# A two-layer hybrid model on one core: the odd mixer's units in another order, and products of constants placed in TensorE's waits

## The chip, the cores and the metric

The kernel runs on one NeuronCore of a Trainium2 chip, in one launch. The metric is the device time in microseconds (us), from the program's start to its end; lower is better. The time before is the median of three runs, 2744.92 us.

TensorE (PE in the profile) multiplies matrices and writes to PSUM, an accumulator memory of eight banks. VectorE (DVE) and ScalarE (ACT) read PSUM and do element-wise work. SyncE (SP) issues the weight transfers. Each engine runs its own list of instructions strictly in the order in which the program wrote it, and waits at counters (semaphores) for the others.

## The reference

A residual stream `x` of 256 tokens by 1024 features passes through two layers of one model and two of another, all in fp32:

```python
# first block: layer 0 uses even_mixer, layer 1 uses odd_mixer; after each a mixture of experts
x = x + mix(rms_norm(x, g))
x = x + hier_moe(rms_norm(x, g), ...)      # 32 experts, hidden width 512, each token uses 2
# second block, twice
h = h + hybrid_mixer(rmsnorm(h, w), ...)
h = h + swiglu(rmsnorm(h, w), ...)
```

The change lies mostly in `odd_mixer`. Its input is projected once (`u = h @ w_in`, 2048 columns) and split into queries, keys, values and an input of a state-space part:

```python
q = apply_rope(rms_norm(q, q_norm), cos, sin)      # 4 heads x 2 halves x 64
k = apply_rope(rms_norm(k, k_norm), cos, sin)
o = softmax(q1 k1) @ v - lam * softmax(q2 k2) @ v  # causal
o_attn = rms_norm(o, subln) * (1 - lam_init)
# S5: complex diagonal recurrence over time, 2048 states, then
z = gelu(real(C @ states) + d_skip * u)
o_ssm = z * sigmoid(z @ w_glu)
return concatenate([o_attn, o_ssm]) @ w_out
```

## The kernel before

Nine stages follow each other: `even`, `moe0`, `odd`, `moe1`, `hyb0`, `ffn0`, `hyb1`, `ffn1`, `fin`. There is no planner: for every stage and every engine a function (`odd_pe`, `odd_act`, `odd_dve` and so on) writes the instructions out in order. At the end of such a function stands a list of calls to small helpers, and this list is the order of the work. A wait names an event of another engine (`K.after("odd normed0")`), or the landing of a weight chunk.

**Weights** come in chunks of 2 MB through a ring of six slots, in a fixed order on the SP queue (`sp_program`). A chunk's transfer is issued when the chunk that held its slot was used, and the chunks behind it wait as well. A mixture of experts reads all its 32 experts, 96 chunks; eight groups of four experts each have four gate chunks, four up chunks and four down chunks.

**PSUM banks** are handed out in turn by `bank`. In `odd` the banks 0 to 3 (`K.low`) and 4 to 7 (`K.high`) are two such rings; who takes a bank waits until the result that was in it four takes ago has been read.

**The mixture of experts** (`moe_pe`): the stream is transposed (L717), the router's product is taken (L785, 36 columns wide), VectorE picks the experts, and TensorE waits for that at `chosen`. Three products that count tokens follow (L789 to L791), then `gather(0)`, which collects the tokens of four experts (L804), then the weights' products: L828 for gate and up, L853 for down, L860 to spread results back over the tokens. The next stage's norm is `norm_pe` (L641): 16 transposes, eight for each half of the tokens, of which four wait for VectorE (`xv`) and four for ScalarE (`xa`). Of a transpose the trace has one record, of every fp32 product two.

**The odd mixer.** On TensorE: `inputs(j)` L1846, a quarter of the S5 input; `states(q)` L1858, a quarter of the states; `outputs(q)` L1867, a quarter of the S5 output, from what VectorE's scans gave; `query_key(i, j)` L1818, half of the queries (i = 0) or keys (i = 1); `squares(i)` L1881 and `turn(i)` L1891, their norm's sums and the rotation for the position coding; `values(t)` L1898. Then for each head h and half of the queries q, numbered n = 2h + q: `scores(n)` L1909, `transposed(n)` L1917, and per head `weighted(h)` L1925 and L1926. `head_squares` L1933 sums for the heads' norm, `gate()` is the product of the S5 gate (again L1818), and `out(n, first)` L1956 the output projection: for each of four blocks of the result four products over the S5 half (`first`), then four over the heads' half.

On VectorE: `turned_in(q)`, six operations over 128x1024; `scanned(q)`, eight scans over time (L2182) and four such operations; `outputs(q)` L2192; `normed(i)` L2200; `roped(i)` from L2207 on; `largest(n)` and `weighed(n)`, the row maxima and the softmax weights; two operations of the GELU (L2268 and L2273, called cubic and gelu); L2282, called mixed, which applies the gate; `heads(j)` L2244. On ScalarE: the readings of PSUM, `rstd(i)`, `exp(n)`, the GELU's square and tanh (L2098, L2102), the gate's tanh (L2115) and `head_rstd(j)` (L2077, L2080).

The waits that matter below: `turn(i)` waits for `normed(i)`; `turned_in(q)` waits for `states(q)` and, before its second half, for `outputs(q-1)` of TensorE; `scores(0)` waits for `roped(1)`; `gate` for gelu; `mixed` for both halves of the gate; `out(n, True)` for mixed; `heads(j)` for `head_rstd(j)`.

## Time and profile before

| | us |
|---|---|
| runs before | 2742.62, 2744.92, 2747.47 (median 2744.92) |
| the profiled execution, its own time | 2738.76 |
| its span, first to last instruction | 2737.0 |
| `even` | 0 to 271.9 |
| `moe0` | 271.9 to 737 |
| `odd` | 737 to 910 |
| `moe1` | 910 to 1375 |
| both hybrid layers, their feed-forwards, the last norm | 1375 to 2737 |
| busy over the span | TensorE 84%, VectorE 46%, ScalarE 34% |
| mean granted TensorE clock | 0.936 |

A clock of 1.00 is 2.4 GHz and 0.50 is 1.2 GHz; the trace shows only these two levels, and a mean between them is a stretch in which it changed. The profile's lines on the granted clock and on the transfers, 40 slices of 68.4 us each, show the stages: in the two mixtures of experts the 16 DMA engines are busy all the time (428 GB/s), in `odd` they are nearly idle for one slice (17 GB/s), and in the second block they run at a third to a half of that rate while TensorE is busy.

The times in the stretches below are us from the span's start. In a timeline a row merges neighbouring instructions of one line: start, length, engine, line, operation, then how many records (x16), and in brackets how long the engine stood idle before it and who released it.

### The profile page before, as it was taken

The page shows a single profiled execution, that of the slowest core. Times are in us where ns is not written, and L with a number is a line of the kernel's source. Part 1 is how long each engine was busy: PE and PEld are TensorE (multiplying, and loading weights), DVE is VectorE, ACT ScalarE, POOL GpSimd, SP SyncE. Part 2 cuts the span into 40 slices and gives each one's busy share as a digit, 9 for nine tenths or more (in the row PEclk, how much of TensorE's full clock was granted, in tenths as well). Part 3 has the DMA queues.
Part 4 walks back from the last instruction along what each step waited for, and adds up shares of the span by engine and source line. Part 5 has one row for each costly group of instructions (what it writes and reads, how often), then busy time and mean ns, then how long its engine had stood idle before and what let it go on. Part 6 is the DMA issues. An engine that isn't in the chain of part 4 may idle for free.

```text
span 2737.0 us, 37411 instructions
## 1 busy us (share of the span) xinstructions
PE 2300.2 (84%) x16364; PEld 1749.6 (64%) x16364; DVE 1263.6 (46%) x1914; ACT 941.2 (34%) x1382; POOL 2.4 (0%) x8
## 2 busy tenths in 40 slices
PE   7877766666696866666599999999999999999999
PEld 6666322211274421122189998999979999989997
DVE  2575321222294211111066568765545656866554
ACT  3133100000113200000055557745444555764543
POOL 0000000000000000000000000000000000000000
PEclk9998888988897988878899999999999999999999
DMA  6101999999905599999954443445544434334452
GB/s 274 62 1 74 400 428 428 428 427 428 416 17 248 244 428 427 427 428 428 427 198 170 149 178 141 154 154 199 182 172 154 167 146 185 130 148 160 180 185 100
DMA packets 47818, 663.18 MB, mean 242 GB/s; under 512 B 5280, under 2 KB 5536, under 8 KB 7584
## 3 DMA queue, kind: packets, MB, share of 16 engines
q1 hardware_dynamic: 47072, 657.39, 59.7%
q8 instruction: 132, 2.16, 0.3%
q0 software_dynamic: 576, 3.32, 0.3%
q14 instruction: 38, 0.31, 0.0%
HBM read 659.64 MB, written 1.05 MB: 241 GB/s over the span
## 4 chain that ended last, share of the span: by engine, by line
PE 54%; DMA 29%; DVE 9%; ACT 7%; issue 2%; SPq 0%; DVEq 0%; ACTq 0%
DMA ring<-w_dram 28%; PE ps L2346 7%; PE ps L2348 7%; PE ps L2347 7%; PE ps L1818 3%; PE ps L1231 2%; PE ps L828 2%; PE ps L2599 2%; PE ps L2600 2%; PE ps L2601 2%; PE ps L853 2%; ACT r L2323 2%; PE ps L3201 1%; PE ps L3199 1%; PE ps L3200 1%
## 5 line engine op out<-in xcount | busy, mean ns | idle before, releaser
L2334 DVE TENSOR_TENSOR r<-ring,r 128x1024 fp32r<-128x1024 f32 (+1 forms) x392 | 505.1, 1301 | 345.9 <-ACT r L2323 345.3
L2346 PE MATMUL ps<-r 128*128 128x256 f32 x2112 | 608.0, 288 | 15.1 <-DVE arena L2933 5.7
L2347 PE MATMUL ps<-r 128*128 128x256 f32 x2112 | 598.2, 283 | 0.0
L2348 PE MATMUL ps<-r 128*128 128x256 f32 x2112 | 598.0, 283 | 0.0
L2323 ACT ACTIVATE r<-ring 128x1024 fp32r<-128x1024 f32 (+1 forms) x392 | 429.5, 1116 | 269.1 <-PE ps L2348 131.8
L828 PE MATMUL ps<-ring,arena 128*32 128x512 f32 x1984 | 297.4, 731 | 207.0 <-DMA ring<-w_dram 206.9
L2346 PEld LDWEIGHTS ps<-r 128*128 128x128 f32 x2112 | 405.5, 192 | 22.8 <-issue 6.7
L2347 PEld LDWEIGHTS ps<-r 128*128 128x128 f32 x2112 | 405.7, 192 | 0.2
L2348 PEld LDWEIGHTS ps<-r 128*128 128x128 f32 x2112 | 405.5, 192 | 0.0
L828 PEld LDWEIGHTS ps<-ring,arena 128*32 128x32 f32 x1984 | 62.1, 121 | 433.0 <-DMA ring<-w_dram 221.2
L1030 DVE TENSOR_TENSOR arena<-ps,arena 128x512 f32<-128x512 f32 x16 | 11.1, 692 | 472.7 <-PE ps L828 472.7
L853 PE MATMUL ps<-ring,arena 128*32 128x512 f32 x1024 | 145.4, 702 | 81.1 <-DMA ring<-w_dram 80.1
L2599 PE MATMUL ps<-arena,r 128*128 128x256 f32 x512 | 145.4, 284 | 0.0
L2600 PE MATMUL ps<-arena,r 128*128 128x256 f32 x512 | 143.9, 281 | 0.0
L853 PEld LDWEIGHTS ps<-ring,arena 128*32 128x32 f32 x1024 | 30.5, 119 | 177.2 <-DMA ring<-w_dram 121.8
L2601 PE MATMUL ps<-arena,r 128*128 128x256 f32 x512 | 143.8, 281 | 0.0
L878 ACT ACTIVATE arena<-ps 128x512 f32<-128x512 f32 x16 | 9.6, 597 | 292.9 <-PE ps L828 292.9
L880 ACT ACTIVATE arena<-ps 128x256 f32<-128x256 f32 x16 | 6.1, 383 | 285.4 <-PE ps L834 285.4
L885 ACT ACTIVATE arena<-ps 128x512 f32<-128x512 f32 x16 | 9.6, 597 | 262.7 <-PE ps L853 262.7
L1038 DVE COPY arena<-ps 128x512 f32<-128x512 f32 x16 | 11.1, 692 | 192.4 <-PE ps L853 192.4
L2599 PEld LDWEIGHTS ps<-arena,r 128*128 128x128 f32 x512 | 96.5, 188 | 1.2 <-issue 0.7
L2600 PEld LDWEIGHTS ps<-arena,r 128*128 128x128 f32 x512 | 96.5, 188 | 0.1
(433 smaller groups left out, 3416.6 us busy)
## 6 DMA issues: line engine op xcount, KB each, us to landing
ring<-w_dram SPq DMA_DIRECT2D x305, 2048.0 KB, 23.7
arena<-w_dram SPq DMA_DIRECT2D x4, 2048.0 KB, 21.9
ring<-w_dram SPq DMA_DIRECT2D x4, 1024.0 KB, 4.9
cst<-w_dram POOLq DMA_DIRECT2D x2, 973.0 KB, 8.2
x<-x_dram SPq DMA_DIRECT2D x1, 1024.0 KB, 7.9
ring<-w_dram SPq DMA_DIRECT2D x2, 512.0 KB, 13.5
out_dram<-x SPq DMA_DIRECT2D x4, 256.0 KB, 2.0
ring<-w_dram SPq DMA_DIRECT2D x1, 768.0 KB, 15.8
```

The costliest lines, as they stand in the source:

```text
L828: r = pe.matmul(p[32 * j:32 * j + 32, :], xg[:, k, j * CAP:(j + 1) * CAP], w[:, kk * 4 + j, :], start=k == 0, stop=k == 7)
L853: r = pe.matmul(ys[n][32 * j:32 * j + 32, :], b.HTr[u][:, k, j * CAP:(j + 1) * CAP], w[:, j, n * 512:(n + 1) * 512], start=k == 0, stop=k ...
L1231: x = pe.matmul(o(c), l[:, c, :], r(c), start=True, stop=True)
L1818: r = pe.matmul(p[:, n * 256:(n + 1) * 256], w[:, k, c0 + n * 128:c0 + n * 128 + 128], rhs[:, k, :], start=k == 0, stop=k == n_k - 1)
L2323: a.activation(hi, w, ACT.Copy).then_inc(*S.up(f"hi {s}"))
L2334: v.tensor_tensor(lo, w, hi.bitcast(F32), SUB).then_inc(*S.up(f"lo {s}", *(["free " + name] if last else [])))
L2346: pe.matmul(out, hi[:, k, :], K.HH[:, k, :], start=k == 0, stop=False)
L2347: pe.matmul(out, hi[:, k, :], K.HL[:, k, :], start=False, stop=False)
L2348: r = pe.matmul(out, lo[:, k, :], K.HH[:, k, :], start=False, stop=k == 7)
L2599: pe.matmul(o, hi[:, k, :], b.YH[:, kk, :], start=kk == 0 and n == 0, stop=False)
L2600: pe.matmul(o, hi[:, k, :], b.YL[:, kk, :], start=False, stop=False)
L2601: r = pe.matmul(o, lo[:, k, :], b.YH[:, kk, :], start=False, stop=kk == 15 and n == 1)
```

## The change

It has two parts. The first writes the odd mixer's list of calls in another order on three engines, cuts the gate's product into its two halves (`gate(0)`, `gate(2)`), cuts the heads' half of the output projection into pairs of products (`out_heads(n, j)`, which needs only `heads(j)`), and puts `normed(i)` between the two rows of scans of `scanned(2)` and `scanned(3)`. The work itself stays the same.

The second adds `warm`, a product of two constants (the identity by a part of a table that begins with it) into a PSUM bank whose contents are overwritten later. It stands ahead of waits: in `norm_pe` (stages `odd`, `hyb0`, `ffn0`, `hyb1`, `ffn1`) once before the wait for `xv0`, 512 or 256 columns wide, and twice, 128 wide, before the wait for `xv1`; three times, 512 wide, before `chosen` in both mixtures of experts; and six times, 512 wide, between the four down chunks of the last group of experts.

```diff
+def warm(K, pe, out):
+
+    n = out.shape[1]
+    pe.matmul(out, K.par("ident", 0, 128), K.par("ident", 0, n), start=True, stop=True)
...
 def norm_pe(K, pe, st):
...
                 p[k] = bank(K, pe, name, of)
             if k == 0:
+                if t == 0 and K.stage_before(st):
+                    warm(K, pe, p[0][:, 0:512 if after_moe(K, st) else 256])
+                elif t and K.stage_before(st):
+                    warm(K, pe, p[6][:, 128:256])
+                    warm(K, pe, p[6][:, 384:512])
                 pe.wait_ge(*K.after(f"{st} xv{t}"))
...
     p = bank(K, pe, st + " pos")
+    for _ in range(3):
+        warm(K, pe, p)
     pe.wait_ge(*K.after(st + " chosen"))
...
         ys = [bank(K, pe, f"{st} y{q}{n}") for n in range(2)]
+        if q == NE // 4 - 1:
+            spare = bank(K, pe, f"{st} o{q}00")
...
             r.then_inc(*S.up("free " + name, f"{st} y{q}"))
+            if q == NE // 4 - 1 and k < 3:
+                warm(K, pe, spare)
+                warm(K, pe, spare)
         for t in range(2):
             for n in range(2):
                 pe.wait_ge(*K.after(f"{st} y{q}{n} read"))
-                p = bank(K, pe, f"{st} o{q}{n}{t}")
+                p = spare if q == NE // 4 - 1 and t == n == 0 else bank(K, pe, f"{st} o{q}{n}{t}")
...
-    def gate():
+    def gate(j):
         pe.wait_ge(*K.landed("glu"))
         pe.wait_ge(*K.after("odd gelu"))
-        for j in (0, 2):
-            for _ in proj_T_pe(K, pe, S, "glu", j * 128, b.Y5, 4, f"odd glu{j}", j == 2, K.high):
-                pass
+        for _ in proj_T_pe(K, pe, S, "glu", j * 128, b.Y5, 4, f"odd glu{j}", j == 2, K.high):
+            pass
...
-    def out(n, first):
+    def out(n, ready, ks):
 
         i, t = divmod(n, 2)
         w = K.chunk(f"odd_out{i}")
-        if first:
+        if ks[0] == 4:
             pe.wait_ge(*K.landed(f"odd_out{i}"))
             acc[n] = bank(K, pe, f"odd out{i}{t}", K.low)
-            pe.wait_ge(*K.after("odd mixed"))
-        else:
-            pe.wait_ge(*K.after("odd heads2"))
-        for k in range(4, 8) if first else range(4):
+        pe.wait_ge(*K.after(ready))
+        for k in ks:
             r = pe.matmul(acc[n], b.OT[:, k, t * 128:(t + 1) * 128], w[:, k, :], start=k == 4, stop=k == 3)
-        if not first:
+        if ks[-1] == 3:
             r.then_inc(*S.up(f"odd out{i}{t}", f"free odd_out{i}"))
+
+    def out_states(n):
+        out(n, "odd mixed", range(4, 8))
+
+    def out_heads(n, j):
+        out(n, f"odd heads{j}", range(j, j + 2))
 
     inputs(0)
     states(0)
@@ -1966,48 +1987,54 @@
     outputs(0)
     query_key(0, 2)
     inputs(3)
+    states(2)
     squares(0)
-    states(2)
+    outputs(1)
     turn(0)
-    outputs(1)
     query_key(1, 0)
     states(3)
     query_key(1, 2)
     outputs(2)
+    squares(1)
     values(0)
-    squares(1)
+    turn(1)
     values(1)
-    turn(1)
     outputs(3)
     scores(0)
     scores(1)
     scores(2)
+    scores(3)
     transposed(0)
-    scores(3)
+    scores(4)
+    gate(0)
     transposed(1)
     weighted(0)
-    scores(4)
+    scores(5)
+    gate(2)
     transposed(2)
-    scores(5)
+    scores(6)
     transposed(3)
     weighted(1)
-    scores(6)
+    scores(7)
+    transposed(4)
     head_squares(0)
-    gate()
-    transposed(4)
-    scores(7)
     transposed(5)
     weighted(2)
-    out(0, True)
+    out_states(0)
     transposed(6)
-    out(1, True)
+    out_states(1)
     transposed(7)
     weighted(3)
-    out(2, True)
+    out_states(2)
     head_squares(2)
-    out(3, True)
-    for n in (0, 2, 1, 3):
-        out(n, False)
+    out_states(3)
+    out_heads(0, 0)
+    out_heads(2, 0)
+    out_heads(0, 2)
+    out_heads(2, 2)
+    for n in (1, 3):
+        out_heads(n, 0)
+        out_heads(n, 2)
 
...
 def odd_act(K, a, st):
...
+    def gate(j):
+        a.wait_ge(*K.after(f"odd glu{j}"))
+        a.activation(b.U5[:, j:j + 2, :], half2(K.high[f"odd glu{j}"]), ACT.Tanh).then_inc(*S.up(f"odd glu{j} read"))
...
     rstd(0)
     query_key(1, 0)
     query_key(1, 2)
+    rstd(1)
     values(0)
-    rstd(1)
     values(1)
-    exp(0)
-    exp(1)
     a.wait_ge(*K.after("odd y3"))
     a.wait_ge(*K.after("odd normed1"))
     a.activation(b.RS, b.Y5, ACT.Square).then_inc(*S.up("odd y squares"))
-    exp(2)
-    transposed(0)
+    exp(0)
+    exp(1)
     a.wait_ge(*K.after("odd cubic"))
     a.activation(b.RS, b.RS, ACT.Tanh, scale=4 * GELU * 16 * 0.044715).then_inc(*S.up("odd tanh"))
+    transposed(0)
+    exp(2)
+    gate(0)
+    transposed(1)
     exp(3)
-    transposed(1)
     weighted(0)
     exp(4)
+    gate(2)
     transposed(2)
+    transposed(3)
     exp(5)
-    transposed(3)
     weighted(1)
     exp(6)
-    head_rstd(0)
-    for j in (0, 2):
-        a.wait_ge(*K.after(f"odd glu{j}"))
-        a.activation(b.U5[:, j:j + 2, :], half2(K.high[f"odd glu{j}"]), ACT.Tanh).then_inc(*S.up(f"odd glu{j} read"))
     transposed(4)
-    exp(7)
     transposed(5)
     weighted(2)
+    exp(7)
+    head_rstd(0)
     transposed(6)
     transposed(7)
     weighted(3)
...
 def odd_dve(K, v, st):
...
         tt(b.TB, b.TB, b.TA, SUB)
         own()
 
-    def scanned(q):
+    def scanned(q, which=None):
 
         Y, Z = b.Y[q % 2], b.Z[q % 2]
         for x in (Y, b.TB):
             for i in range(4):
                 r = bc(s.rho[:, q * 4 + i:q * 4 + i + 1], [128, 256])
                 v.tensor_tensor_scan(x[:, i, :], r, x[:, i, :], 0.0, MUL, ADD).then_inc(*S.up())
+            if x is Y and which is not None:
+                normed(which)
         own()
         tt(b.TA, Y, s.CS[q], MUL)
         v.scalar_tensor_tensor(out=Z, in0=b.TB, scalar=-1.0, in1=s.SN[q], op0=MUL, op1=MUL).then_inc(*S.up())
@@ -2249,28 +2281,26 @@
     turned_in(1)
     scanned(1)
     outputs(0)
-    normed(0)
     turned_in(2)
+    outputs(1)
+    scanned(2, 0)
     roped(0)
-    scanned(2)
-    outputs(1)
     turned_in(3)
-    scanned(3)
     outputs(2)
-    normed(1)
+    scanned(3, 1)
     roped(1)
     outputs(3)
     largest(0)
     largest(1)
-    weighed(0)
-    largest(2)
     v.wait_ge(*K.after("odd y squares"))
     v.scalar_tensor_tensor(out=b.RS, in0=b.RS, scalar=1.0 / (16 * 0.044715), in1=b.Y5, op0=ADD, op1=MUL).then_inc(
         *S.up("odd cubic"))
+    weighed(0)
+    largest(2)
+    v.wait_ge(*K.after("odd tanh"))
+    v.scalar_tensor_tensor(out=b.Y5, in0=b.RS, scalar=1.0, in1=b.Y5, op0=ADD, op1=MUL).then_inc(*S.up("odd gelu"))
     weighed(1)
     largest(3)
-    v.wait_ge(*K.after("odd tanh"))
-    v.scalar_tensor_tensor(out=b.Y5, in0=b.RS, scalar=1.0, in1=b.Y5, op0=ADD, op1=MUL).then_inc(*S.up("odd gelu"))
     weighed(2)
     largest(4)
     weighed(3)
```

What the lists make of it, at three places. The rows are the programs' instructions in order, without times: line, operation, what it writes and reads, the shape of the output, and how many alike follow. Lines of the changed file are its own.

TensorE, the projections of the odd mixer, from `inputs(3)` (L1846) on, before: `squares(0)` L1881, `states(2)` L1858, `turn(0)` L1891, `outputs(1)` L1867, then `query_key`, `states(3)`, `query_key`, `outputs(2)`, `values(0)` L1898, `squares(1)`, `values(1)`:

```order
L1846 MATMUL ps<-ring 128x256 x8
L1881 MATMUL ps<-arena,pp 128x256 x4
L1858 MATMUL ps<-arena,ring 128x256 x8
L1891 MATMUL ps<-arena,cst 128x256 x4
L1867 MATMUL ps<-arena,ring 32x256 x16
L1818 MATMUL ps<-ring 128x256 x16
L1858 MATMUL ps<-arena,ring 128x256 x8
L1818 MATMUL ps<-ring 128x256 x16
L1867 MATMUL ps<-arena,ring 32x256 x16
L1898 MATMUL ps<-ring 128x512 x8
L1881 MATMUL ps<-arena,pp 128x256 x4
L1898 MATMUL ps<-ring 128x512 x8
```

and now, the same helpers at L1864, L1899, L1876, L1909, L1885, L1836 and L1916:

```order
L1864 MATMUL ps<-ring 128x256 x8
L1876 MATMUL ps<-arena,ring 128x256 x8
L1899 MATMUL ps<-arena,pp 128x256 x4
L1885 MATMUL ps<-arena,ring 32x256 x16
L1909 MATMUL ps<-arena,cst 128x256 x4
L1836 MATMUL ps<-ring 128x256 x16
L1876 MATMUL ps<-arena,ring 128x256 x8
L1836 MATMUL ps<-ring 128x256 x16
L1885 MATMUL ps<-arena,ring 32x256 x16
L1899 MATMUL ps<-arena,pp 128x256 x4
L1916 MATMUL ps<-ring 128x512 x8
L1909 MATMUL ps<-arena,cst 128x256 x4
```

`states(2)` (L1876) stands ahead of `squares(0)` (L1899), `outputs(1)` (L1885) ahead of `turn(0)` (L1909), and the second `turn` ahead of the second `values`.

VectorE, from the end of `outputs(0)` (L2192) to the scans of the third quarter (L2182), before; L2200 is `normed(0)`, L2207 the start of `roped(0)`:

```order
L2192 SCALAR_TENSOR_TENSOR arena<-arena,cst,ps 128x256
L2200 SCALAR_TENSOR_TENSOR arena<-arena,pp 128x1024
L2134 TENSOR_TENSOR arena<-ps,arena 128x1024 x2
L2134 TENSOR_TENSOR arena<-arena 128x1024
L2134 TENSOR_TENSOR arena<-ps,arena 128x1024 x2
L2134 TENSOR_TENSOR arena<-arena 128x1024
L2207 TENSOR_TENSOR arena<-ps,cst 128x512 x2
L2134 TENSOR_TENSOR arena<-arena,cst 128x1024
L2134 TENSOR_TENSOR arena<-arena 128x1024
L2182 SCALAR_TENSOR_TENSOR arena<-cst,arena 128x256 x8
```

and now, with `outputs` at L2224, scans at L2212 and `normed(0)` at L2232; `roped(0)` is at L2239:

```order
L2224 SCALAR_TENSOR_TENSOR arena<-arena,cst,ps 128x256
L2164 TENSOR_TENSOR arena<-ps,arena 128x1024 x2
L2164 TENSOR_TENSOR arena<-arena 128x1024
L2164 TENSOR_TENSOR arena<-ps,arena 128x1024 x2
L2164 TENSOR_TENSOR arena<-arena 128x1024
L2224 SCALAR_TENSOR_TENSOR arena<-arena,cst,ps 128x256
L2212 SCALAR_TENSOR_TENSOR arena<-cst,arena 128x256 x4
L2232 SCALAR_TENSOR_TENSOR arena<-arena,pp 128x1024
L2212 SCALAR_TENSOR_TENSOR arena<-cst,arena 128x256 x4
L2164 TENSOR_TENSOR arena<-arena 128x1024
L2217 SCALAR_TENSOR_TENSOR arena<-arena 128x1024
L2218 SCALAR_TENSOR_TENSOR arena<-arena 128x1024
```

`normed(0)` was the first thing after `outputs(0)`; it now stands seven operations and four scans later, and `roped(0)` behind all eight scans and their four products.

TensorE, attention, from `scores(6)` on, before: `head_squares(0)` L1933, the whole gate L1818, transposes L1917, `weighted(2)` L1925 and L1926, `out(0, True)` L1956:

```order
L1909 MATMUL ps<-arena 128x128 x2
L1933 MATMUL ps<-arena,pp 128x256 x2
L1818 MATMUL ps<-arena,ring 128x256 x16
L1917 MATMUL ps<-pp,arena 128x128
L1909 MATMUL ps<-arena 128x256 x2
L1917 MATMUL ps<-pp,arena 128x128 x2
L1925 MATMUL ps<-arena 128x256
L1926 MATMUL ps<-arena 128x128
L1956 MATMUL ps<-ring,arena 128x512 x4
```

and now, from `scores(3)` on, with `scores` at L1927, transposes L1935, the gate's halves L1836, `weighted(0)` at L1943 and L1944:

```order
L1927 MATMUL ps<-arena 128x256 x2
L1935 MATMUL ps<-pp,arena 128x128
L1927 MATMUL ps<-arena 128x128 x2
L1836 MATMUL ps<-arena,ring 128x256 x8
L1935 MATMUL ps<-pp,arena 128x128 x2
L1943 MATMUL ps<-arena 128x256
L1944 MATMUL ps<-arena 128x128
L1927 MATMUL ps<-arena 128x256 x2
L1836 MATMUL ps<-arena,ring 128x256 x8
L1935 MATMUL ps<-pp,arena 128x128
L1927 MATMUL ps<-arena 128x128 x2
```

The gate's first half stands between the transposes of the first head, the second half ahead of those of the second head; before, both stood behind the second head.

## Rows read from the trace of the kernel before

**Rows 1.** The page, chain that ended last, by engine.
```profile
PE 54%; DMA 29%; DVE 9%; ACT 7%; issue 2%; SPq 0%; DVEq 0%; ACTq 0%
```

**Rows 2.** Stretches: length, busy and instructions by engine, PE clock, DMA share, GB/s.
```profile
841.00:910.00 69.00, 54.58 (x166) 30.32 (x163) 24.79 (x67) 28.47 (x72) 0.00 (x0) 0.80 0.61 252
880.00:905.00 25.00, 24.29 (x61) 11.11 (x61) 2.13 (x3) 8.73 (x16) 0.00 (x0) 0.97 0.02 9
921.00:930.00 9.00, 9.00 (x64) 7.16 (x68) 4.12 (x17) 0.00 (x0) 0.00 (x0) 0.73 0.01 4
```

**Rows 3.** Timeline of PE, projections of the odd mixer (start, length, ..., idle before).
```profile
782.36 1.92 PE L1881 MATMUL ps<-arena,pp 128*128 128x256 f32 x4 [3.06 <-DVE arena L2192]
...
792.64 7.17 PE L1818 MATMUL ps<-ring 128*128 128x256 f32 x32
...
818.94 1.89 PE L1881 MATMUL ps<-arena,pp 128*128 128x256 f32 x8
826.80 8.88 PE L1898 MATMUL ps<-ring 128*128 128x512 f32 x16 [5.98 <-DVE arena L2192]
...
840.67 0.93 PE L1909 MATMUL ps<-arena 64*128 64x128 f32 x8 [1.40 <-DVE arena L2134]
```

**Rows 4.** Timeline of DVE, the same stretch.
```profile
772.49 4.77 DVE L2182 TENSOR_TENSOR_SCAN arena<-cst,arena 128x256 f32<-128x256 f32 x8
...
781.83 0.48 DVE L2192 SCALAR_TENSOR_TENSOR arena<-arena,cst,ps 128x256 f32<-128x256 f32 x1
787.49 1.28 DVE L2200 SCALAR_TENSOR_TENSOR arena<-arena,pp 128x1024 f32<-128x1024 f32 x1 [5.18 <-ACT arena L2046]
788.69 2.35 DVE L2134 TENSOR_TENSOR arena<-ps,arena 128x1024 f32<-128x1024 f32 x2
...
836.58 0.69 DVE L2207 TENSOR_TENSOR arena<-ps,cst 128x512 f32<-128x512 f32 x1 [8.64 <-PE ps L1891]
```

**Rows 5.** Timeline of PE, attention, gate and output projection.
```profile
862.94 7.84 PE L1818 MATMUL ps<-arena,ring 128*128 128x256 f32 x32
...
875.73 1.19 PE L1925 MATMUL ps<-arena 128*128 128x256 f32 x2 [3.84 <-ACT arena L2065]
...
892.29 17.74 PE L1956 MATMUL ps<-ring,arena 128*128 128x512 f32 x40
```

**Rows 6.** Timeline of DVE, the wait for the gate.
```profile
871.44 1.23 DVE L2282 SCALAR_TENSOR_TENSOR arena<-arena 128x1024 f32<-128x1024 f32 x1 [8.13 <-ACT arena L2115]
```

**Rows 7.** Stretch of DVE: largest(4), weighed(3), largest(5), weighed(4).
```profile
853.60:858.10 4.50, 4.21 (x14) 0.50 1.01 433
```

**Rows 8.** Stretch of ACT: head_rstd(0), four instructions.
```profile
863.20:867.20 4.00, 3.88 (x4) 0.84 1.01 426
```

**Rows 9.** Timeline of ACT, the first of them.
```profile
863.20 1.28 ACT L2077 ACT_TABLE_LOAD   x1
```

**Rows 10.** Stretches of PE: length, busy, granted clock, DMA share, GB/s.
```profile
277.50:287.50 10.00, 6.27 (x28) 0.50 1.00 425
728.00:731.40 3.40, 3.34 (x16) 0.51 0.97 408
844.00:864.50 20.50, 12.53 (x38) 0.50 1.01 429
```

**Rows 11.** Timeline of PE, first mixture of experts: after the router, gather(0), gather(1).
```profile
280.41 0.60 PE L789 MATMUL ps<-arena,pp 128*128 128x32 f32 x2 [3.29 <-DVE arena L970]
...
282.69 6.16 PE L804 MATMUL ps<-arena 128*128 128x128 f32 x32 [0.82 <-issue]
...
304.46 3.74 PE L804 MATMUL ps<-arena 128*128 128x128 f32 x32
```

**Rows 12.** Timeline of PE, its last group: two down chunks, the next norm.
```profile
723.17 1.92 PE L853 MATMUL ps<-ring,arena 128*32 128x512 f32 x16 [1.59 <-DMA ring<-w_dram]
728.06 3.53 PE L853 MATMUL ps<-ring,arena 128*32 128x512 f32 x16 [2.97 <-DMA ring<-w_dram]
...
738.84 1.50 PE L641 MATMUL ps<-pp,arena 128*128 128x128 f32 x12 [0.70 <-ACT arena L576]
```

## The prediction

> **What bounds the kernel now.** I read the chain of waits first: TensorE holds 54% of it, transfers 29% [rows 1]. The transfers' share lies in the two mixtures of experts, whose weights run at full rate. So I asked what lies between them, the odd mixer, and whether time saved there survives. Stretches of the page answer the second question: between 880 and 905 us the DMA engines are idle (share 0.02), and again between 921 and 930 (0.01) [rows 2]. The next weights wait there for a slot, which TensorE frees when it reaches the experts. What the odd mixer ends earlier, `moe1` starts and ends earlier, as long as it is less than these 34 us.
>
> Then the timelines, engine against engine. In the projections both engines wait in turn. TensorE waits 3.06 us at 782.36 inside `squares(0)`, whose second bank is free only after VectorE's `outputs(0)`, with `states(2)` queued behind it; and 5.98 us at 826.80, `values(1)`, for the bank that VectorE's `outputs(2)` reads [rows 3]. VectorE waits 5.18 us for the norm's factors before `normed(0)` and 8.64 us before `roped(1)`, for `turn(1)`, which stands behind `values(1)` [rows 4]. In attention TensorE does the whole gate in one piece, 7.84 us, and meanwhile VectorE waits 8.13 us for it at `mixed` [rows 5, 6]; after that TensorE waits 3.84 us for the third head [rows 5]. Only then does the output projection begin. From 841 to 910 TensorE is busy 54.6 us at a mean clock of 0.80 [rows 2]; between 844 and 864.5 it is at 0.50 throughout [rows 10].
>
> **The projections.** All before `squares(0)` is as it was. I follow the new lists with the old durations: 3.5 us for `inputs` or `states` (half of the 7.17 us of a `query_key`), 1.9 us for `outputs`, 1.75 for `squares` or `turn`, 7.0 for `values` at full clock [rows 3]; on VectorE 1.15 to 1.18 us for an operation over 128x1024, so 7.1 for `turned_in`, 4.8 for eight scans, 9.4 for `scanned` [rows 4].
>
> `states(2)` now ends at 781.8, before VectorE is through with `outputs(0)` at 782.3. VectorE therefore goes straight into `turned_in(2)`: the 5.18 us go. It ends at 789.5, `outputs(1)` at 789.9, four scans at 792.3, and `normed(0)` at 793.4. This is 5 us later than before, and it is the new wait: TensorE is through with `outputs(1)` at 785.5, and `turn(0)` blocks it for 8 us. Everything behind it is queued: `query_key(1, 0)`, `states(3)`, `query_key(1, 2)`, `outputs(2)`. The clock will have fallen; I add 1.4 us. From there TensorE alone sets the pace: turn 1.75, query_key 7, states 3.5, query_key 7, outputs 1.9, squares 1.75, values 7, turn 1.75, values 7, outputs 1.9, in all 40.5, plus 1.4: it ends at 835.4. VectorE fits beside it: `scanned(2)` ends at 800.5, `roped(0)` at 804.2, then it waits for `states(3)` to 807.1 and in the middle of `turned_in(3)` for `outputs(2)` to 816.0, so `normed(1)` is done at 823.6, `scanned(3)` at 830.6, `roped(1)` at 834.3. `scores(0)` starts at 835.4 instead of 840.67 [rows 3]: 5.3 us gained. The margins are 1.2 us (`turn(1)` wants `normed(1)` at 824.8) and 1.1 us (`roped(1)`). Ends: 1.4 us less if the clock stays up; 3.5 more if it is low until the first `query_key` is done.
>
> **Attention.** VectorE's work up to `mixed` is `largest` and `weighed` for n = 0 to 5, one more `largest`, and three GELU and gate products. Two pairs of the former take 4.5 us [rows 7], so 13.5, plus 1.1, plus three of 1.2 [rows 6] make 18.2 us. It is ready at 835.9, and would end at 854.1 without a wait. I find 5 us of waits. Half of the gate, 3.5 us at full clock and 7 at the low one, starts at 843.0 when gelu is there; TensorE has been nearly idle by then, and I take 5.7 us, to 848.7. `transposed(1)` stands behind it, and behind that on ScalarE `exp(3)`, so VectorE waits some 3 us before `weighed(3)`. The second half of the gate ends at 854.5, and `scores(6)`, behind it, costs 0.7 more, `exp(5)` behind the gate's tanh another 0.7. `mixed` is done at 859.4, and the output projection begins at 860.0, with `weighted(2)` just ahead. Before, it began at 877.3.
>
> From there: four `out_states` and four times `out_heads`, 3.44 us for four products (17.74 us for five times as many at full clock [rows 5]), 27.5 us; the transposes, `weighted(3)` and `head_squares(2)` 1.8; and about 1.6 of waiting for `weighed(7)`. For ScalarE does `head_rstd(0)` after `exp(7)`, 3.9 us [rows 8], `heads(0)` waits for that, and `weighed(7)` stands behind `heads(0)`. That gives 890.9, plus 1.2 for low clock at the start of `out_states(0)`: 892.1. `head_rstd(2)` lies beside `out_states(3)` as before. Against the old 910.0 this is 17.9 us less for the whole stage, of which 12.6 in attention. Ends: 1.2 less with the clock up; 8 more if both halves of the gate (another 1.3 and 3.5) and more of the output projection run low.
>
> Here a page speaks against the new order. Rows first: ScalarE's load of tables takes 1.28 us [rows 9], and the two loads and two operations of `head_rstd` 3.9 in all [rows 8]. The Trainium skill, "ScalarE: Activation LUTs", section "What ACT_TABLE_LOAD costs", adds about 1.4 us of draining to each switch, 2.66 in all. By that rule `head_rstd(0)` would hold `weighed(7)` 2.8 us longer, and the stage would end 2.8 us later. The trace has no such gap.
>
> **The products of constants.** A 512-column fp32 product takes 0.86 us at 1.00 (a fourth of 3.44) and twice that at 0.50.
> - Ahead of `chosen`, three: 2.6 us warm, 5.2 cold, in a wait of 3.29 us [rows 11]. The clock was at 0.50 from 277.5 to 287.5 [rows 10]; `gather(0)` took 6.16 us, `gather(1)` at full clock 3.74 [rows 11]. Best case: hidden, gather 2.4 us shorter, the small products 0.4. Worst: all at the low level, 1.9 us late, and gather no faster. I take 1.0 us gained, nearer the best, because three dense products in a row are what preceded each rise of the clock here. Two stages: 2.0.
> - In the last group of experts, two after each of three down chunks, 1.72 us in a gap of 3 [rows 12]. The last chunk ran at 0.50 [rows 10] and took 3.53 us instead of 1.92 [rows 12]; `moe1` shows the same. Gain 1.6 and 1.4 in this execution. If the first chunk starts cold, 3.5 + 3.5 us exceed the 4.9 between chunks, which is caught up by the fourth. Ends: nothing, and these 3.0.
> - In the norms, one in a wait of over a microsecond: free. Two of 128 columns, 0.43 us together, stand ahead of `xv1`, which in `odd` is long there: the eight transposes behind them move 0.43 us [rows 12], and the chain with them. In `hyb0` 0 to 0.9, I take 0.4, since the cutting of weights lies beside. In `ffn0`, `hyb1`, `ffn1` `xv1` comes last: nothing.
>
> **Sum.** Against the profiled execution's 2738.76: -17.9 (odd) -2.0 -3.0 +0.4 +0.4 = -22.1. The median of the runs lies 6.2 us above the profiled one, and whether a last chunk meets the low clock will vary from run to run, so I count half of the 3.0: 2744.92 - 20.6 = 2724.
>
> **Rivals.**
> A. The constants run cold and late. For: the clock was low just there. Against: it rises after dense work [rows 10, 11]. Both `chosen` 1.9 late instead of 1.0 early, and no gain at the last chunks: 2724 + 5.8 + 1.5 + 1 for the norms = 2732.
> B. Attention keeps most of its length, because the gate's half ahead of `transposed(1)` holds back every later softmax at low clock, and only the projections gain: of the 12.6 us 3 remain. For: the cold stretch [rows 10]. 2724 + 9.6 = 2734.
> C. The stream of weights takes the gain: `moe1` ends when it did. Against: 34 us of idle DMA [rows 2]. Only the first mixture's gain would stay: 2742.
> D. Slower. From 842 to the end of the stage the clock stays at 0.50, because the work is chopped into pieces between waits. TensorE has 40 us of work there, which then costs 40 more, less the 3.4 already counted: 2724 + 36.6 = 2761. It decides from 21 us of the work at the low level beyond those counted. For: in this stretch it was low for 20.5 us [rows 10]. Against: the gate and the output projection are long dense pieces, and each ran at full clock after its beginning. The Trainium skill, "TensorE: Matmul & The Clock Gate", section "A second HAM failure mode: psum-queue depth-cycling", tells of a kernel that idled briefly between groups and swung between the levels; by that rule this rival would be likelier than I make it.
>
> **How the numbers follow.** Forecast 0.70, A 0.12, B 0.09, C 0.05, D 0.04. The forecast's own ends are 2717 (everything at full clock) and 2736 (the projections' 3.5 and the attention's 8 us); A and B lie inside. I give 2716 to 2737. A measurement of this kernel can tell about 0.2%, 5.5 us. Forecast, A and B are faster by more, and a few of their tails are not: faster 0.91, within 0.2% 0.05 (C), slower 0.04 (D).
>
> **What would show it.** In the profile after: VectorE without a wait before `turned_in(2)`; TensorE idle for 8 us before `turn(0)`; `scores(0)` 5 us sooner after the norm than before; the gate in two pieces with VectorE's wait at `mixed` gone and one of about 3 us before `weighed(3)`; the output projection starting 17 us earlier; gather(0) near 3.7 us; the last down chunk at 1.9 us. It is wrong if `mixed` comes later than 25 us after `scores(0)`, or if `moe1` is longer than before.

## The result and the profile after

| | before | after |
|---|---|---|
| median of the runs timed together, us | 2743.77 (4 runs, 2742.60 to 2747.47) | 2716.53 (4 runs, 2712.74 to 2718.73) |
| the profiled execution, its own time | 2738.76 | 2717.73 |
| its span | 2737.0 | 2715.9 |
| mean granted TensorE clock | 0.936 | 0.943 |

The ratio after to before is 0.9897, with a 95% interval of 0.988 to 0.9914, so the change takes 24 to 33 us off. The medians differ by 27.2 us, the two profiled executions by 21.0. Forecast were 20.6 and 22.1. The direction came as forecast, and so did the odd mixer; the products of constants gave more than was counted. The gain against the median is a third larger than forecast, and 2716.53 lies half a microsecond above the lower end of the range.

The timeline of TensorE in the kernel after, from the odd mixer's projections to the output projection:

```profile
780.73 1.89 PE L1899 MATMUL ps<-arena,pp 128*128 128x256 f32 x8
782.55 1.93 PE L1885 MATMUL ps<-arena,ring 128*32 128x256 f32 x32
792.49 3.75 PE L1909 MATMUL ps<-arena,cst 128*128 128x256 f32 x8 [8.01 <-issue]
796.03 7.21 PE L1836 MATMUL ps<-ring 128*128 128x256 f32 x32
...
834.64 0.93 PE L1927 MATMUL ps<-arena 64*128 64x128 f32 x8
...
841.97 6.42 PE L1836 MATMUL ps<-arena,ring 128*128 128x256 f32 x16 [1.25 <-issue]
...
850.85 3.72 PE L1836 MATMUL ps<-arena,ring 128*128 128x256 f32 x16
...
860.20 3.60 PE L1971 MATMUL ps<-ring,arena 128*128 128x512 f32 x8
...
868.03 0.41 PE L1935 MATMUL ps<-pp,arena 128*128 128x128 f32 x2 [0.69 <-DVE arena L2270]
...
891.20 1.92 PE L728 MATMUL ps<-pp,x 128*128 128x128 f32 x16
```

The new wait is there: 8.01 us before `turn(0)` (L1909). The profile names no releaser for it ("issue"), but by the list `turn(0)` waits for `normed(0)`, and VectorE ends that at 792.38, 0.11 us before `turn(0)` starts. The gate (L1836) stands in two pieces of 6.42 and 3.72 us where it was one of 7.84 [rows 5]. The output projection (L1971) begins at 860.20; it began at 877.14.

VectorE's timeline after, at `outputs(0)` and `turned_in(2)`, then its longer waits further on:

```profile
780.82 0.47 DVE L2224 SCALAR_TENSOR_TENSOR arena<-arena,cst,ps 128x256 f32<-128x256 f32 x1
781.22 2.34 DVE L2164 TENSOR_TENSOR arena<-ps,arena 128x1024 f32<-128x1024 f32 x2
...
791.12 1.26 DVE L2232 SCALAR_TENSOR_TENSOR arena<-arena,pp 128x1024 f32<-128x1024 f32 x1
...
806.73 2.35 DVE L2164 TENSOR_TENSOR arena<-ps,arena 128x1024 f32<-128x1024 f32 x2 [3.74 <-PE ps L1876]
815.53 2.36 DVE L2164 TENSOR_TENSOR arena<-ps,arena 128x1024 f32<-128x1024 f32 x2 [5.19 <-PE ps L1885]
...
850.30 0.17 DVE L2265 RECIPROCAL cst<-cst 128x2 f32<-128x2 f32 x1 [4.02 <-ACT arena L2085]
...
866.08 0.75 DVE L2276 SCALAR_TENSOR_TENSOR arena<-arena,cst 128x512 f32<-128x512 f32 x1 [4.53 <-ACT arena L2107]
```

The wait of 5.18 us behind `outputs(0)` [rows 4] is gone, and so are the one of 8.64 before `roped(1)` [rows 4] and the one of 8.13 at `mixed` [rows 6]. What has come instead in attention is 4.02 us before `weighed(3)` and 4.53 us before `heads(0)` (L2276), which waits for `head_rstd(0)`. The waits of 3.74 and 5.19 cost nothing, since TensorE works without a pause from 792.49 to the end of `outputs(3)`.

ScalarE's timeline after, `head_rstd(0)` (L2104 and L2107):

```profile
862.04 1.28 ACT L2104 ACT_TABLE_LOAD   x1
863.34 0.69 ACT L2104 ACTIVATE arena<-ps,pp 128x512 f32<-128x512 f32 x1
864.04 1.28 ACT L2107 ACT_TABLE_LOAD   x1
865.34 0.63 ACT L2107 ACTIVATE arena<-arena 128x512 f32<-128x512 f32 x1
```

Stretches of TensorE after: length, busy and records, granted clock, share of the DMA engines, GB/s:

```profile
279.80:289.00 9.20, 7.85 (x54) 1.00 1.02 432
785.00:797.00 12.00, 4.51 (x12) 0.72 0.00 0
...
840.00:848.00 8.00, 6.72 (x20) 0.57 1.01 426
848.00:890.00 42.00, 38.83 (x127) 1.00 0.70 293
...
902.00:905.50 3.50, 3.50 (x19) 0.52 0.02 9
```

In the first mixture of experts nothing is at the low level from 279.8 on, where it was from 277.5 to 287.5 [rows 10]. In attention the low level lasts some 7 us in 840 to 848; before, it lasted 20.5 [rows 10] and another 6.8 us from 874.7 to 881.5. Over the whole stage, from `inputs(0)` to `moe1`, the mean granted clock is 0.95 instead of 0.89, and TensorE is busy 135.2 us instead of 143.4 with the same instructions. So about 8 of the 17.7 us between these two profiles are the same work at a higher clock, and the rest is less waiting. The kernel with the new order alone (below) has the same two numbers, 0.95 and 134.8 us.

TensorE's timeline after, first mixture: the three products of constants (L630, two records each) and `gather(0)` (L817); the same in the second mixture; then the last group's down chunks (L868):

```profile
279.81 2.82 PE L630 MATMUL ps<-pp 128*128 128x512 f32 x6
...
284.84 3.81 PE L817 MATMUL ps<-arena 128*128 128x128 f32 x32 [0.82 <-issue]
...
896.45 2.82 PE L630 MATMUL ps<-pp 128*128 128x512 f32 x6
...
901.48 5.44 PE L817 MATMUL ps<-arena 128*128 128x128 f32 x32 [0.82 <-issue]
```

```profile
713.63 2.96 PE L868 MATMUL ps<-ring,arena 128*32 128x512 f32 x16 [1.52 <-DMA ring<-w_dram]
716.52 2.60 PE L630 MATMUL ps<-pp 128*128 128x512 f32 x4
...
728.22 1.92 PE L868 MATMUL ps<-ring,arena 128*32 128x512 f32 x16 [1.05 <-DMA ring<-w_dram]
```

`gather(0)` went from 6.16 to 3.81 us [rows 11], in the second mixture only to 5.44. The last down chunk went from 3.53 to 1.92 [rows 12].

Before and after by stage, in us, from the starts of the same instructions in the traces. Two more executions of the kernel before were profiled later, and the column of before has all three:

| stretch | before, three executions | after |
|---|---|---|
| `even`, up to the first mixture | 271.7, 275.6, 272.5 | 274.6 |
| first mixture to its first weights' product | 17.44, 17.72, 17.34 | 14.39 |
| from there to `inputs(0)` of `odd` | 451.60, 452.51, 451.04 | 450.79 |
| `odd`, from `inputs(0)` to the transposes of `moe1` | 169.11, 169.07, 169.62 | 151.46 |
| second mixture to its first weights' product | 17.51, 17.25, 17.48 | 16.01 |
| from there to the first product of `hyb0` | 452.63, 452.92, 452.92 | 451.32 |
| the second block to the end | 1357.00, 1359.28, 1359.41 | 1357.37 |

`even` differs by up to 4 us between executions of one kernel, and the change touches nothing in it.

### The profile page after: what moved, and what is told of

It reads as the page before. It is cut to its first block, busy times and chain, and to the rows that moved or that the text cites. A ratio compares the mean times of both kernels' runs of the same rounds, so it can differ in the third digit from the quotient of the medians.

```text
span 2715.9 us, 37536 instructions
## 1 busy us (share of the span) xinstructions
PE 2311.1 (85%) x16430; PEld 1755.8 (65%) x16430; DVE 1263.2 (47%) x1914; ACT 941.1 (35%) x1382; POOL 2.4 (0%) x8
## 3 DMA queue, kind: packets, MB, share of 16 engines
q0 software_dynamic: 576, 3.32, 0.3%
## 4 chain that ended last, share of the span: by engine, by line
PE 56%; DMA 29%; ACT 7%; DVE 6%; issue 2%; SPq 0%; DVEq 0%; ACTq 0%
DMA ring<-w_dram 29%; PE ps L2376 7%; PE ps L2377 7%; PE ps L2378 7%; PE ps L1836 4%; PE ps L1249 2%; PE ps L841 2%; PE ps L2629 2%; PE ps L2630 2%; PE ps L2631 2%; ACT r L2353 2%; PE ps L868 2%; PE ps L3229 1%; PE ps L3231 1%; PE ps L3230 1%
## 5 line engine op out<-in xcount | busy, mean ns | idle before, releaser
L868 PE MATMUL ps<-ring,arena 128*32 128x512 f32 x1024 | 141.1, 684 | 67.6 <-DMA ring<-w_dram 66.6
L868 PEld LDWEIGHTS ps<-ring,arena 128*32 128x32 f32 x1024 | 30.2, 117 | 158.9 <-DMA ring<-w_dram 102.7
```

Of the source, the lines that this page charges most:

```text
L868: r = pe.matmul(ys[n][32 * j:32 * j + 32, :], b.HTr[u][:, k, j * CAP:(j + 1) * CAP], w[:, j, n * 512:(n + 1) * 512], start=k == 0, stop=k ...
```

## The experiments

The order of the lists and the products of constants are taken apart first, then the constants by place; then come the waits that the new order left.

**The new order alone.** The changed kernel with every call of `warm` out, and with the first spreading product's bank taken where it was before.

```diff
-                    warm(K, pe, p[0][:, 0:512 if after_moe(K, st) else 256])
...
-                    warm(K, pe, p[6][:, 128:256])
-                    warm(K, pe, p[6][:, 384:512])
...
-    for _ in range(3):
-        warm(K, pe, p)
...
-                warm(K, pe, spare)
-                warm(K, pe, spare)
```

> The changed kernel without any product of constants. Measured for the whole change: 27.2 us less by the medians (0.9897), where 20.6 were forecast. Theory A (the constants are worth more than the 3 us I gave them): the order alone gives the 17.5 us that the timelines show for the odd stage, ratio 0.9936, some 2726 us. Theory B (the constants are sized right, the order gives more than its stage shows): 24 us, ratio 0.9912, some 2720 us.

Measured: 2724.25 (2722.67 to 2727.09) against 2741.48 for before on the same chip, ratio 0.9933 [0.992, 0.9946], which is 18.4 us less (14.8 to 21.9). From `inputs(0)` to `moe1` it is 150.74 us, against 151.46 with the constants. So the order is worth what was forecast for it, 17.9 us, and no more. It also shortens the stretch from `moe1`'s transposes to its first weights' product without any constants, to 16.55 us from some 17.4.

One thing was not expected. The timeline of TensorE in this kernel, last down chunk of the second mixture and the four products that spread it (L866), and the stretch around them:

```profile
1349.02 3.64 PE L859 MATMUL ps<-ring,arena 128*32 128x512 f32 x16 [1.74 <-DMA ring<-w_dram]
1353.38 6.17 PE L866 MATMUL ps<-arena 128*128 128x512 f32 x8 [0.72 <-ACT arena L891]
```

```profile
1342.00:1363.00 21.00, 14.36 (x51) 0.67 0.90 383
```

The clock is low at the end of `moe1`, and its last four products take 6.17 us instead of 3.70. From the first weights' product to `hyb0` it is 455.49 us, 2.7 more than in the three executions of before. The new order is not shown to be the cause. The kernel without the six products (below) has the new order and nothing in these waits either, and there the four products take 3.70 us. And one of the later executions of the kernel before has the same in its first mixture:

```profile
735.70 5.44 PE L860 MATMUL ps<-arena 128*128 128x512 f32 x8 [0.70 <-ACT arena L885]
```

Without the six products the four ran partly at the low level in two of ten places (two mixtures in each of five profiles); with them, in none of eighteen.

**The products of constants alone.** The kernel before with all of `warm`, its lists in the old order.

```diff
+def warm(K, pe, out):
+    n = out.shape[1]
+    pe.matmul(out, K.par("ident", 0, 128), K.par("ident", 0, n), start=True, stop=True)
...
+    for _ in range(3):
+        warm(K, pe, p)
...
+            if q == NE // 4 - 1 and k < 3:
+                warm(K, pe, spare)
+                warm(K, pe, spare)
```

> The kernel before with all products of constants, and its old order. Theory A: 9 to 10 us less, ratio 0.9965. Theory B: 3 us less, ratio 0.999. If both parts act independently, this ratio and that of the order alone multiply to 0.9897.

Measured: 2734.72 (2729.51 to 2736.99), ratio 0.9967 [0.9955, 0.9979]: 9.1 us less (5.8 to 12.3). The prediction counted 2.0 + 1.5 - 0.8 = 2.7. The two ratios multiply to 0.9900, the whole change gave 0.9897: the parts add up within the intervals, and this one was mis-sized. By stages, against the mean of the three executions of before, it has 3.1 and 1.4 us in the two stretches to the first weights' product, 1.3 and 1.5 in the rest of the two mixtures, and 0.7 in the odd mixer.

**Without the six in the last group.**

```diff
-            if q == NE // 4 - 1 and k < 3:
-                warm(K, pe, spare)
-                warm(K, pe, spare)
```

> The changed kernel without the six products in the last group of experts. I sized them at 3.0 us in the profiled execution and half of it in the median. Theory A, if they are the underrated part: 4 us or more slower than the changed kernel (ratio to before 0.9912 or more), and last down chunks at 3.4 us. Theory B: 1.5 us slower, ratio 0.9902.

Measured: 2721.61 (2718.63 to 2721.93), ratio 0.992 [0.9907, 0.9933], 5.1 us above the whole change by medians, 6.3 by the ratios to before. The two intervals overlap at the edge, so the runs alone do not prove this size; the stages show the place. The last down chunk of the second mixture takes again over 3 us:

```profile
1346.38 3.38 PE L866 MATMUL ps<-ring,arena 128*32 128x512 f32 x16 [2.97 <-DMA ring<-w_dram]
```

From the first weights' product to this row's start it is 438.82 us; in all fourteen profiled executions of this case that distance lies between 438.49 and 438.85, with the six products and without. The transfers set it. What the six products give is only what comes behind the last transfer: the last chunk's own time, the spreading products, the norm. To `hyb0` it is 454.06 us here, 451.3 to 451.6 in the nine executions with the six. Of these 2.7 us the last chunk has 1.5 and its later start 0.3. The rest, 1.0, is a pause of 2.83 us of TensorE ahead of the norm, in this kernel's profile only, for which the profile names no cause; it is not shown to belong to the six products. What is regular is the chunk: 3.15 to 3.64 us in all ten places without the six, 1.92 in all eighteen with them, so 1.2 to 1.7 us in each mixture.

**Without the three ahead of `chosen`.**

```diff
     p = bank(K, pe, st + " pos")
-    for _ in range(3):
-        warm(K, pe, p)
     pe.wait_ge(*K.after(st + " chosen"))
```

> The changed kernel without the three products ahead of chosen, in both mixtures. Sized at 1.0 us each. Theory A, if these are the underrated part: 2.5 to 3 us each, so 5 to 6 slower than the changed kernel, ratio to before about 0.9917, and gather(0) at 6.2 us again. Theory B: 2 us slower, ratio 0.9904.

Measured: 2719.67 (2716.68 to 2724.58), ratio 0.9921 [0.9908, 0.9933], 3.1 us above the whole change by medians, 6.6 by the ratios to before. By stages: 17.41 us to the first weights' product instead of 14.39 in the first mixture, 16.70 instead of 16.01 in the second. The size is inconclusive by the runs alone, since the intervals overlap. The profiles of all kernels show the place, and that the gain is not the same each time. The first mixture's stretch is 17.3 to 17.7 us in the five without these products; in the eight with three of them it is 14.4 in six and 15.3 in two. The second's is 16.55 and 16.70 in the two with the new order and no product there; with three it is 16.0 in three, 15.3 in two and 14.4 in two.

**One product instead of three there.**

```diff
-    for _ in range(3):
+    for _ in range(1):
         warm(K, pe, p)
```

> The changed kernel with one product ahead of chosen instead of three. If the clock holds because TensorE has any dense work between the router and gather: gather(0) stays near 3.8 us in the first mixture, time as the changed kernel, ratio 0.9897. If it needs them all: gather(0) at 5.4 to 6.2 us in both and 3 to 4.5 us slower than the changed kernel, ratio 0.991.

Measured: 2716.64 (2713.89 to 2719.01), ratio 0.9903 [0.9886, 0.9919]: the same time as with three. TensorE's timeline, first mixture:

```profile
280.68 1.10 PE L630 MATMUL ps<-pp 128*128 128x512 f32 x2
...
285.71 5.15 PE L817 MATMUL ps<-arena 128*128 128x128 f32 x32 [0.82 <-issue]
```

The stage has 15.72 us to its first weights' product, between 14.39 with three and 17.41 with none, and `gather(0)` 5.15 between 3.81 and some 6.2. In the first mixture one product gives about half of the gain; in the second the stretch is 16.54 us, as without any. The runs cannot tell 1.3 us.

**Without those in the norms.**

```diff
-                if t == 0 and K.stage_before(st):
-                    warm(K, pe, p[0][:, 0:512 if after_moe(K, st) else 256])
-                elif t and K.stage_before(st):
-                    warm(K, pe, p[6][:, 128:256])
-                    warm(K, pe, p[6][:, 384:512])
```

> The changed kernel without the products in the five norms. So far: the order alone gives 0.9933, all products alone 0.9967; removing those before chosen costs 4.5 us, those of the last group 5. Theory A1 (the two groups are all of it, the norms' cost a little, as I priced them at 0.8 us): 0.5 to 1 us faster than the changed kernel, ratio to before 0.9895. Rival A2 (the norms' products also help, because in some executions the clock falls in a norm and the work behind it starts at 0.50): 1 to 3 us slower, ratio 0.9905.

Measured: 2716.44 (2714.14 to 2719.12), ratio 0.9904 [0.9887, 0.992]: no difference from the whole change. The norm ahead of `odd`, first in this kernel (transposes L647, then `inputs(0)`), then in the kernel after (L652):

```profile
738.04 0.63 PE L647 MATMUL ps<-pp,arena 128*128 128x128 f32 x4 [1.48 <-DVE arena L609]
739.37 2.79 PE L647 MATMUL ps<-pp,arena 128*128 128x128 f32 x12 [0.70 <-ACT arena L576]
741.96 4.05 PE L1859 MATMUL ps<-ring 128*128 128x256 f32 x16
```

```profile
735.95 0.66 PE L652 MATMUL ps<-pp,arena 128*128 128x128 f32 x4 [0.53 <-DVE arena L609]
737.38 0.63 PE L652 MATMUL ps<-pp,arena 128*128 128x128 f32 x4 [0.77 <-ACT arena L576]
737.85 0.61 PE L630 MATMUL ps<-pp 128*128 128x128 f32 x4
738.30 1.04 PE L652 MATMUL ps<-pp,arena 128*128 128x128 f32 x8
739.74 3.69 PE L1864 MATMUL ps<-ring 128*128 128x256 f32 x16 [0.41 <-DVE ring L664]
```

Without them twelve transposes run partly at the low level here, 2.79 us; with them four and eight take 1.67 and the two small products lie between. But the clock does not fall in every norm without them. The same twelve transposes in the kernel with the new order alone, which has no products in the norms either:

```profile
741.13 1.51 PE L647 MATMUL ps<-pp,arena 128*128 128x128 f32 x12 [0.72 <-ACT arena L576]
```

From the last spreading product to `inputs(0)` it is 4.6 to 4.7 us in three of the five profiles without these products, 5.2 and 5.4 in the two where the clock fell, and 5.2 in all nine with them. So in `odd` they cost the 0.4 to 0.5 us that were forecast, except where they keep the clock up. Ahead of `hyb0` it is 6.4 us with them, and 6.3 to 6.4 without.

This kernel also shows the other end of the products ahead of `chosen`. They stand directly behind the router, which ran at full clock, and still the clock fell while they ran; so it did in the first mixture of the next kernel, with `query_key(1, 0)` ahead of `turn(0)`, of which this is the timeline of TensorE:

```profile
277.94 4.52 PE L630 MATMUL ps<-pp 128*128 128x512 f32 x6
...
283.87 3.81 PE L817 MATMUL ps<-arena 128*128 128x128 f32 x32 [0.82 <-issue]
```

The three take 4.52 us instead of 2.82 and end after VectorE's choice is there, and the counting products start 1.0 us later than in the kernel after (9.6 instead of 8.6 us behind the first transpose of the mixture). `gather(0)` is at full clock all the same. These are the places where the stretch is 15.3 us.

**`query_key(1, 0)` ahead of `turn(0)`.** The half of the keys needs nothing that `turn(0)` waits for, and it takes 7.2 us, about the length of the new wait.

```diff
     outputs(1)
-    turn(0)
     query_key(1, 0)
+    turn(0)
     states(3)
```

> The changed kernel with query_key(1, 0) ahead of turn(0) on TensorE: the 8 us that TensorE waits for normed(0) are filled with 7 us of work. If TensorE alone sets the pace behind that wait, as I predicted from the lists: the stage 6 to 8 us shorter, ratio to before 0.987. Rival: ScalarE may read the keys only after roped(0), so their bank stays held and outputs(2) and squares(1) wait for it, VectorE becomes the bound, and 3 us or less are gained, ratio 0.989.

Measured: 2704.56 (2703.30 to 2708.74), ratio 0.9865 [0.9848, 0.9883]: 37 us less than before, and 12.0 less than the changed kernel by medians, 8.8 by the ratios to before (11.9 and 10.5 less than the kernel without the norms' products and the one with the late gate, which ran beside it on the same chip). TensorE's timeline in this kernel, and below it two stretches with their clocks:

```profile
782.51 7.17 PE L1836 MATMUL ps<-ring 128*128 128x256 f32 x32
790.60 1.97 PE L1909 MATMUL ps<-arena,cst 128*128 128x256 f32 x8 [0.91 <-issue]
...
823.97 0.93 PE L1927 MATMUL ps<-arena 64*128 64x128 f32 x8
...
831.31 5.40 PE L1836 MATMUL ps<-arena,ring 128*128 128x256 f32 x16 [0.90 <-issue]
```

```profile
782.50:800.00 17.50, 16.59 (x80) 1.00 0.00 0
829.00:837.00 8.00, 6.79 (x23) 0.64 1.02 430
```

The wait is 0.91 us instead of 8.01, and `turn(0)` takes 1.97 instead of 3.75, for the clock stays up. From `inputs(0)` to `scores(0)` it is 86.13 us against 94.90 (7.1 of the wait, 1.8 of `turn(0)`), and from `inputs(0)` to `moe1` 141.68 against 151.46, 9.8 us less. So the forecast wait was real, it was on the path, and nothing behind it hid it. Of VectorE's waits of 3.74 and 5.19 us the first went with it and 0.23 are left of the second: they were an echo of TensorE's. The rival, by which the bank of the keys would have held TensorE up and 3 us or less were gained, did not come.

**The first half of the gate behind `transposed(1)`.**

```diff
     scores(4)
-    gate(0)
     transposed(1)
+    gate(0)
     weighted(0)
     scores(5)
```

(the same on ScalarE's list, behind `exp(3)`.)

> The changed kernel with the gate's first half behind transposed(1) instead of ahead of it, on TensorE and ScalarE. The wait of 4.0 us before weighed(3) should go. If that wait is on the path to mixed: out_states(0) 2 to 3 us earlier, ratio to before 0.989. Rival: the gate then ends later by the same amount and mixed waits for it, no change against the changed kernel, 0.99.

Measured: 2715.08 (2713.22 to 2715.94), ratio 0.9901 [0.9884, 0.9918]: no difference from the whole change. VectorE's timeline in this kernel:

```profile
846.44 0.69 DVE L2252 SCALAR_TENSOR_TENSOR arena<-ps,cst 128x512 f32<-128x512 f32 x1 [3.21 <-PE ps L1927]
850.62 0.42 DVE L2252 SCALAR_TENSOR_TENSOR arena<-ps,cst 128x256 f32<-128x256 f32 x1 [1.72 <-PE ps L1927]
```

The wait of 4.02 us before `weighed(3)` is gone, and one of 3.21 stands before `largest(5)`: now `scores(5)` is queued behind the half of the gate. From `scores(0)` to the output projection it is 25.13 us, against 25.56; the kernels with the gate in its first place have 24.3 to 25.6, so this is no gain. In both places tried, something that VectorE needs is behind the half of the gate.

**All three rearrangements.** The two above, and `weighed(7)` ahead of `heads(0)`, which no longer waits then for `head_rstd(0)`.

```diff
     weighed(6)
-    heads(0)
     weighed(7)
+    heads(0)
     heads(2)
```

> Both of these, and weighed(7) ahead of heads(0) on VectorE, so that the last transposes no longer wait for ScalarE's head_rstd(0). If the three waits are independent: 7 + 2.5 + 1 us less than the changed kernel, some 2705 us, ratio 0.986. If they overlap: 0.988.

Measured: 2705.40 (2703.61 to 2705.73), ratio 0.9865 [0.9848, 0.9881]: what the first of them gives alone. The third shortens the output projection by 0.9 us (30.12 against 31.00), less than the runs can tell.

**`query_key(1, 0)` first and `weighed(7)` first,** without the move of the gate.

```diff
-    turn(0)
     query_key(1, 0)
+    turn(0)
...
-    heads(0)
     weighed(7)
+    heads(0)
```

> The changed kernel with query_key(1, 0) ahead of turn(0), and weighed(7) ahead of heads(0). The first alone gave 2704.6 us, ratio 0.9865. If weighed(7) is worth what the trace of all three together shows, 0.9 us from the start of the output projection to the next stage: 2703.5 us, ratio 0.9861. Rival: the order of weighed(7) is hidden behind out_states(1), no difference.

Measured: 2707.12 (2701.38 to 2710.05), ratio 0.9875 [0.9859, 0.9892]. No gain over 2704.56. The 0.9 us of the output projection are there again (30.13).

**The kernel before, profiled twice more.** No edit.

> The kernel before, unchanged, one more profiled execution, to see where its profiled execution of 2738.8 us was shorter than the median of 2743.8. Theory C (the forecast's own basis was a lucky execution): this one takes 2741 us or more, with the even stage 2 to 4 us longer than 271.7 and, in the second mixture, the last group's end later, 449 to 451 us from its first expert product to the next norm instead of 447.7. Rival D: the stages repeat to half a microsecond, and the 5 us lie outside the span or spread over the second block.

> The same once more. Theory C: again 2741 us or more, by the even stage and the last groups. Rival D: as the first.

Measured: 2746.14 and 2742.12, one execution each. They are 7.4 and 3.4 us longer than the profiled execution on which the sum was made. Of the 7.4, `even` has 3.9 and the second block 2.3; of the 3.4, 0.8 and 2.4. Each of the stretches that the change touches differs by at most 0.9 us from the first profile. So the profiled execution was short mostly where the change does nothing. The expected later end of the last group did not come: from the first weights' product of `moe1` to the next norm it is 448.0 us in both, against 447.7.

The version to keep is the one with `query_key(1, 0)` ahead of `turn(0)`: 2704.56 us, faster than both kernels. The two that add more moves to it cannot be told from it.

## Why the prediction was right, and where it was not

**Projections: right.** Forecast was VectorE straight into `turned_in(2)`, 8 us of waiting before `turn(0)`, 1.4 us for the clock, and `scores(0)` 5.3 us sooner after the norm. The trace has no wait, 8.01 us, 1.8 us (3.75 against 1.97 at full clock), and 94.90 us from `inputs(0)` to `scores(0)` against 99.92, 5.0 sooner.

**Attention: right.** Forecast were `out_states(0)` 24.6 us behind `scores(0)`, a first half of the gate of 5.7 us and a wait of about 3 before `weighed(3)`. Measured were 25.56, 6.42 and 4.02. The loss of 1.0 us was made up behind it: from `out_states(0)` to `moe1` forecast were 32.1 us, measured 31.00, since the 1.2 us for a low clock did not come and the 1.6 us of waiting for `weighed(7)` came to 0.69. From `inputs(0)` on the stage shrank by 17.8 us against the mean of the three executions of before; forecast were 17.9, and the kernel with the new order alone took off 18.4 (14.8 to 21.9).

By an estimate from the Trainium skill, "ScalarE: Activation LUTs", section "What ACT_TABLE_LOAD costs", two drains of about 1.4 us would have made this 2.8 us longer. The trace does not agree: `head_rstd(0)` takes 3.9 us from 862.04 to 865.97 with its loads of 1.28 us back to back with the work, as before [rows 8].

**The stream of weights: right.** The second mixture begins earlier and ends earlier, and the distance from its first weights' product to its last down chunk is the same in every kernel (438.5 to 438.9 us).

**The clock in attention: right.** Rival D wanted 0.50 up to the end of the stage; it is 1.00 from 848 to 890. Some 7 us in 840 to 848 remain.

**The step that failed: the sum for the products of constants.** It counted 2.7 us, and the runs of the constants alone gave 9.1 (5.8 to 12.3). What they do was seen rightly; the sizes of two terms were too small. In the table, less is a gain:

| term | counted | measured, by stages |
|---|---|---|
| ahead of `chosen`, first mixture | -1.0 | -3.1 in six of eight profiles (17.5 to 14.4), -2.2 in two (15.3) |
| the same, second mixture | -1.0 | -1.4 with the old order (17.4 to 16.0); with the new one -0.6 in this execution (16.6 to 16.0), -0.6 to -2.2 in all |
| last group, both mixtures | -1.5, half of 3.0 | -3.0, from the last chunks alone (some 3.4 to 1.92 each) |
| norms | +0.8 | +0.5 in `odd` where the clock stays up without them (three of five profiles), none in `hyb0` |
| together | -2.7 | -7.0 with the old order |

- For `chosen` the sum took 1.0 us out of a span from 1.9 lost to 2.8 gained. In the kernel after, and in most of the others, the first mixture got the best end and a little more: the three products follow the router at full clock, and the stretch from 279.8 to 289 is at 1.00 throughout. The worst end came nowhere, but a part of it did: in four of sixteen places the clock fell inside the three products, which then ended 1.0 us late, and the gather was fast even so. The two effects stand in one place together, where the sum had them as one or the other. The reason given for the choice, three dense products ahead of each rise of the clock, is not what the trace shows either: at 830.3 us the clock rose two products into `values(1)`.
- In the second mixture the kernel after is 1.4 us shorter, but some 0.8 of this comes from the new order: 16.55 us without any constants. The sum had no term for it.
- Halving the last group's 3.0 us was the wrong correction. All three executions of before have a cold last chunk in both mixtures (3.53, 3.15, 3.24 and 3.32, 3.60, 3.47 us), every kernel with the six products has 1.92. The gain was regular; it needed no discount. What may be saved at times behind that chunk, up to 2.5 us in the four spreading products, was not counted; two places of ten do not show that it is due to the six.
- The norms' +0.4 in `odd` was right where the clock stays up without them; the +0.4 in `hyb0` did not come.

Of the 9.1 us the stages place 7.0 in these four terms. The profile of the constants alone has another 0.7 in the odd mixer, where none of them stands. The remainder lies within the interval and has no place.

**The basis.** The sum was made on a profiled execution 6.2 us below the median and carried over to the median unchanged. That was right: `even`, which the change does not touch, and the second block, where its products in the norms show nothing, made it short. It also explains why the difference of the two profiled executions (21.0) looks like a hit on the forecast 22.1: `even` was 2.9 us longer in the one after, and that hides the larger gain of the constants. By the stages that the change touches, against the mean of the three executions of before, it is 17.8 + 3.1 + 0.9 + 1.4 + 1.5 = 24.7 us. The 27.2 of the medians leave 2.5 us without a place; 24.7 lies within the interval (24 to 33), and the second block's 1357 to 1359 us are too unsteady to tell. That stays open.

What the prediction did not say at all is that its own new wait could be filled. It named what is queued behind `turn(0)`, `query_key(1, 0)` first, and priced the idle at 8 us and 1.4. The entry at the head of that queue needed nothing that was late.

## What to carry to other kernels

When a list's new order makes a blocking wait, look at the entries queued behind it for one that needs nothing late and is about as long: moving one call gave 9 to 12 us, where the whole reordering had given 18. Products of constants in a wait paid here where work that had run cold stood on the path behind them, and a bound for them is read from the same rows at both levels of the clock; they did not keep the clock up every time, so one profile does not give their size. Where transfers set the pace, only what comes behind the last transfer counts. Profile the kernel before more than once, and compare by stages: totals of single executions differed here by 7 us, 6 of them in places where the change does nothing that shows.
